# First block of a two-block transformer on one core: the pair stage's jobs, flips and head sums spread over other slots, head factors and key scalings on GpSimd

## The reference

```
h = rms_norm(x) @ w_in       -> h_cq, h_ckv, h_kr, h_dq, h_dk, h_dv, h_gq, h_gk, h_gv
MLA   q_a = rms_norm(h_cq) @ w_uq          6 heads of 64 + 32 (the 32 with rope)
      k_a, v_a = rms_norm(h_ckv) @ w_ukv   keys get the shared rope part h_kr
diff  q_b, k_b, v_b                        4 heads, two 64-wide maps each, values 128 wide
      a = softmax(q0 k0) - lam * softmax(q1 k1);  o_b = rms_norm(a v) * (1 - lambda_init)
GQA   q_c (6 heads), k_c, v_c (2 heads)    axial rope
every q and k of every head: rms_norm(.) * gain, then rope, before the scores
x = x + concat(o_a, o_b, o_c) @ w_o
x = x + (silu(gate) * up) @ w_down,  gate, up = rms_norm(x) @ w_gate_up
```

## Time and profile before

| | us |
|---|---|
| median of three runs | 1777.88 (1773.91 to 1779.11) |
| the profiled execution | 1779.98 |
| its span, first to last instruction | 1778.2 |
| TensorE matmul busy | 1718.4 (97%) |
| VectorE busy | 1198.3 (67%) |
| ScalarE busy | 901.3 (51%) |
| GpSimd busy | 93.9 (5%) |
| mean granted TensorE clock | 0.983 |

### The profile page before, as it was taken

The page is one execution under the profiler, slowest core; times in us unless marked ns, Lnnn a source line. Parts: engine busy times, 40 slices in busy tenths (PEclk is TensorE's granted clock), DMA queues, the critical chain, the costliest instruction groups (busy, mean ns, idle before and its releaser), DMA issues.

```text
span 1778.2 us, 31852 instructions
## 1 busy us (share of the span) xinstructions
PE 1718.4 (97%) x13590; PEld 1655.6 (93%) x13590; DVE 1198.3 (67%) x1752; ACT 901.3 (51%) x1374; POOL 93.9 (5%) x60
## 2 busy tenths in 40 slices
PE   9878999999779999999999999999999999999997
PEld 9867999999769999999999999999999999899997
DVE  5875676647766666367767758984567758769863
ACT  5565544444476444353544765544534545655542
POOL 2000000020000000030000100000200000010000
PEclk9988999999889999999999999999999999999999
DMA  7220565544203654465334434644444345335550
GB/s 279 90 97 13 190 200 186 184 163 151 98 31 129 215 178 166 177 212 176 135 131 166 156 131 157 215 163 160 176 161 163 119 152 191 130 128 193 196 179 35
DMA packets 52830, 274.31 MB, mean 154 GB/s; under 512 B 6096, under 2 KB 6736, under 8 KB 52560
## 3 DMA queue, kind: packets, MB, share of 16 engines
q1 hardware_dynamic: 52544, 271.22, 44.8%
q10 hardware_dynamic: 144, 1.05, 0.2%
HBM read 271.19 MB, written 1.05 MB: 153 GB/s over the span
## 4 chain that ended last, share of the span: by engine, by line
PE 86%; DVE 9%; ACT 2%; issue 2%; ACTq 0%; DVEq 0%
PE bank L774 17%; PE bank L777 17%; PE bank L776 17%; PE scores L774 3%; PE scores L777 3%; PE scores L776 3%; PE bank L783 2%; PE bank L785 2%; PE bank L786 2%; PE heads L774 2%; DVE weights_lo L646 2%; PE heads L776 2%; PE heads L777 2%; PE scores L1094 1%; ACT probs L1167 1%
## 5 line engine op out<-in xcount | busy, mean ns | idle before, releaser
L646 DVE TENSOR_TENSOR weights_lo<-raw,weights_hi 128x1536 fp32r<-128x1536 f32 (+2 forms) x344 | 584.2, 1715 | 257.3 <-ACT weights_hi L635 257.0
L635 ACT ACTIVATE weights_hi<-raw 128x1536 fp32r<-128x1536 f32 (+4 forms) x352 | 499.7, 1438 | 229.0 <-PE bank L777 95.2
L774 PE MATMUL bank<-x_hi,weights_lo 128*128 128x256 f32 (+1 forms) x1600 | 458.9, 287 | 0.4 <-DVE weights_lo L646 0.4
L777 PE MATMUL bank<-x_hi,weights_hi 128*128 128x256 f32 (+1 forms) x1600 | 452.6, 283 | 0.0
L776 PE MATMUL bank<-x_lo,weights_hi 128*128 128x256 f32 (+1 forms) x1600 | 452.5, 283 | 0.0
L774 PEld LDWEIGHTS bank<-x_hi,weights_lo 128*128 128x128 f32 (+1 forms) x1600 | 304.8, 191 | 5.8 <-issue 4.8
L776 PEld LDWEIGHTS bank<-x_lo,weights_hi 128*128 128x128 f32 (+1 forms) x1600 | 304.9, 191 | 2.0 <-issue 2.0
L777 PEld LDWEIGHTS bank<-x_hi,weights_hi 128*128 128x128 f32 (+1 forms) x1600 | 304.9, 191 | 0.0
L776 PE MATMUL bank<-hidden_lo,weights_hi 128*128 128x256 f32 x704 | 198.2, 282 | 0.0
L774 PE MATMUL bank<-hidden_hi,weights_lo 128*128 128x256 f32 x704 | 198.2, 282 | 0.0
L777 PE MATMUL bank<-hidden_hi,weights_hi 128*128 128x256 f32 x704 | 198.2, 282 | 0.0
(11 more groups left out here) (410 smaller groups left out, 3435.3 us busy)
## 6 DMA issues: line engine op xcount, KB each, us to landing
raw<-in_w_b SPq DMA_DIRECT2D x194, 768.0 KB, 4.2
raw<-in_w_a SPq DMA_DIRECT2D x120, 768.0 KB, 4.3
raw<-in_w_a SPq DMA_DIRECT2D x16, 512.0 KB, 3.5
raw<-in_w_b SPq DMA_DIRECT2D x10, 512.0 KB, 4.0
raw<-in_w_b SPq DMA_DIRECT2D x2, 752.0 KB, 4.7
raw<-in_w_a SPq DMA_DIRECT2D x2, 736.0 KB, 8.1
raw<-in_w_b SPq DMA_DIRECT2D x2, 720.0 KB, 4.8
raw<-in_w_a SPq DMA_DIRECT2D x2, 672.0 KB, 7.0
```

Of the source, the lines that this page charges most:

```text
L635: nc.scalar.activation(whi[c % SPLIT][:, 0:n], raw[c % RAW][:, 0:n], ACT.Copy).then_inc(*s.mark("weights_hi", c))
L646: nc.vector.tensor_tensor(wlo[c % SPLIT][:, 0:n], raw[c % RAW][:, 0:n], whi[c % SPLIT][:, 0:n].bitcast(F32), ALU.subtract).then_inc(*s.mar ...
L774: ins = nc.tensor.matmul(dst, wl, xh, start=start, stop=False, skip_group_check=skip)
L777: ins = nc.tensor.matmul(dst, wh, xh, start=False, stop=stop, skip_group_check=skip)
```

## The change

The order of the pair stage is written anew. dv0's values and the splits that belong to its job come before slot 0's pair_in, dv1's values move inside slot 1, the flip of dk1 moves to after slot 1, uk and uq jobs and their ropes move up to one slot ahead, the flips of uk0 to uk2 and uq0 move to after slots 4 and 5, the head sums and the flips of uq1 and uq2 to after slot 6. The uq jobs no longer split chunks ahead; an entry ("chunks", 19) after slot 6 splits chunk 19, so chunk 20 is split with part0's job.

The roots "mla" become two groups, "uk" and "uq". For both, and for the head sums' factor, ScalarE's square root and VectorE's reciprocal go; GpSimd raises the means to the power -0.5 instead, with one `tensor_tensor` against a tile of -0.5. The mean of the head sums is now written by VectorE from PSUM. The three multiplications of MLA keys by their factors go from VectorE to GpSimd. "ready" of an MLA pair is the flip of its queries, which is now the later one. GpSimd waits at the start for VectorE's memsets.

```diff
@@ -470,6 +470,7 @@
         QUIET = place("quiet", 8)
+        HALF = place("minus_half", 16)
         _, na = gain_places(0)
@@ -957,7 +958,7 @@
         QK_NAMES = [q[0] for q in qk_jobs]
-        ROOTS = {"early": (0, 4), "late": (4, 6), "mla": (6, 12)}
+        ROOTS = {"early": (0, 4), "late": (4, 6), "uk": (6, 9), "uq": (9, 12)}
         ROOTS_OF = {name: g for g, (a, b) in ROOTS.items() for name in QK_NAMES[a:b]}
@@ -968,13 +969,13 @@
                     ("job", "dk1"), ("flip", "dk0"), ("scale", "gk"), ("rope", "dq1"), ("flip", "g1"), ("rope", "dk1"), ("job", "dv0"), ("flip", "dq1"),
-                    ("flip", "gk"), ("pair_in", 0), ("roots", "late"), ("scale", "dk1"), ("lambda", 0), ("split", "dv0")]
-        inside = {2: [("rope", "uk0")], 3: [("rope", "uk2")], 4: [("rope", "uq0")], 5: [("rope", "uq2")],
-                  6: [("dif_sum", 0), ("flip", "uq1"), ("flip", "uq2"), ("roots", "mla")] + [("scale", f"uk{i}") for i in range(3)], 7: [("flip", "uk2"), ("dif_spread", 0)],
+                    ("flip", "gk"), ("values", "dv0"), ("pair_in", 0), ("roots", "late"), ("scale", "dk1"), ("lambda", 0)]
+        inside = {1: [("values", "dv1")], 2: [("rope", "uk0"), ("rope", "uk1")], 3: [("rope", "uk2"), ("roots", "uk")] + [("scale", f"uk{i}") for i in range(3)],
+                  4: [("rope", "uq0"), ("rope", "uq1")], 5: [("rope", "uq2")], 6: [("roots", "uq")], 7: [("dif_spread", 0)],
                   12: [("root_table", "o"), ("job", "o3")]}
-        after = {0: [("values", "dv0"), ("flip", "dk1"), ("job", "dv1")], 1: [("values", "dv1"), ("job", "uk0"), ("job", "uk1")], 2: [("rope", "uk1"), ("job", "uk2")],
-                 3: [("job", "uq0"), ("job", "uq1")], 4: [("rope", "uq1"), ("job", "uq2"), ("flip", "uq0")],
-                 6: [("flip", "uk0"), ("flip", "uk1")], 7: [("dif_out", 0)],
+        after = {0: [("job", "dv1")], 1: [("flip", "dk1"), ("job", "uk0"), ("job", "uk1")], 2: [("job", "uk2"), ("job", "uq0")], 3: [("job", "uq1")],
+                 4: [("job", "uq2"), ("flip", "uk0")], 5: [("flip", "uk1"), ("flip", "uk2"), ("flip", "uq0")],
+                 6: [("dif_sum", 0), ("flip", "uq1"), ("flip", "uq2"), ("chunks", 19)], 7: [("dif_out", 0)],
                  8: [("angles", 0), ("job", "part0")], 9: [("job", "part1")], 10: [("job", "part2")]}
@@ -1061,7 +1062,7 @@
                     "v": [(slice(c * 64, c * 64 + 64), lambda kt, h=2 * j + c: MV[:, kt, h * MLA_V:(h + 1) * MLA_V]) for c in range(2)],
-                    "ready": ("qk_flip", f"uk{j}"), "values": ("values", f"uk{j}")}
+                    "ready": ("qk_flip", f"uq{j}"), "values": ("values", f"uk{j}")}
 
@@ -1125,6 +1126,8 @@
                     dve.wait_ge(*s.at(l, "map_exp", 2 * i - 1))
+                if i == DIF_H + GQA_H // 2:
+                    dve.wait_ge(*s.at(l, "by_pool", "uq"))
                 for c in range(2):
@@ -1188,6 +1191,7 @@
         SUMS_BY_ACT = ("dq0", "dk0", "g0")
+        NO_SPLITS = ("uq0", "uq1", "uq2")
 
@@ -1209,7 +1213,9 @@
             ps = start_use(pl, pe, l, f"flip_{name}")
-            if name[1] == "k":
+            if name[:2] == "uk":
+                pe.wait_ge(*s.at(l, "by_pool", name))
+            elif name[1] == "k":
                 pe.wait_ge(*s.at(l, "qk_rope", name))
@@ -1376,12 +1382,7 @@
             st = stage(at)
-            if name[0] == "u":
-                dve.wait_ge(*s.at(l, "qk_raw", name))
-                k = heads_of(st[:, 0:4 * MLA_QK], MLA_QK)
-                f = HFACT[:, i, 0:4].rearrange("p (h x) -> p h x", x=1).to_broadcast([P, 4, MLA_QK])
-                ins = nc.vector.tensor_tensor(k, k, f, ALU.mult)
-            elif name == "gk":
+            if name == "gk":
                 dve.wait_ge(*s.at(l, "qk_sum", job))
@@ -1394,6 +1395,33 @@
             ins.then_inc(*s.mark("qk_rope", name))
+
+        def pool_power(dst, src, half):
+
+            return nc.gpsimd.tensor_tensor(dst, src, half, ALU.pow)
+
+        def pool_factor(pl, pool, l, name):
+
+            s = A
+            a, b = ROOTS[name]
+            pool.wait_ge(*s.at(l, "qk_mean", QK_NAMES[b - 1]))
+            pool_power(HFACT[:, a:b, 0:4], HROOT[:, a:b, 0:4], HALF[:, 0:12].rearrange("p (a n) -> p a n", n=4)).then_inc(*s.mark("by_pool", name))
+
+        def pool_scale(pl, pool, l, name):
+
+            s = A
+            i, at, _ = qk_place(name)
+            pool.wait_ge(*s.at(l, "by_pool", "uk"))
+            pool.wait_ge(*s.at(l, "qk_raw", name))
+            k = heads_of(stage(at)[:, 0:4 * MLA_QK], MLA_QK)
+            f = HFACT[:, i, 0:4].rearrange("p (h x) -> p h x", x=1).to_broadcast([P, 4, MLA_QK])
+            nc.gpsimd.tensor_tensor(k, k, f, ALU.mult).then_inc(*s.mark("by_pool", name))
+
+        def pool_dif_factor(pl, pool, l):
+
+            s = A
+            pool.wait_ge(*s.at(l, "dif_root"))
+            pool_power(OFACT[:, :], OROOT[:, :], HALF[:, :]).then_inc(*s.mark("by_pool", "dif"))
 
@@ -1446,7 +1474,7 @@
                 elif kind == "dif_spread":
-                    pe.wait_ge(*s.at(l, "dif_factor"))
+                    pe.wait_ge(*s.at(l, "by_pool", "dif"))
                     for j in range(2):
@@ -1533,10 +1561,10 @@
                     load_root_table(name)
-                if kind == "split":
-                    split_hi(pl, act, l, pl.last_chunk(name) + 2)
+                if kind == "chunks":
+                    split_hi(pl, act, l, name)
                 if kind == "job":
-                    if name != "dv0":
+                    if name not in NO_SPLITS:
                         split_hi(pl, act, l, pl.last_chunk(name) + 2)
@@ -1565,17 +1593,12 @@
                     nc.scalar.activation(NROOT[:, :], NROOT[:, :], ACT.Sqrt).then_inc(*s.mark("norm_root", "latent"))
-                elif kind == "roots":
+                elif kind == "roots" and name in ("early", "late"):
                     a, b = ROOTS[name]
                     act.wait_ge(*s.at(l, "qk_mean", QK_NAMES[b - 1]))
-                    n = 4 if name == "mla" else 8
-                    nc.scalar.activation(HROOT[:, a:b, 0:n], HROOT[:, a:b, 0:n], ACT.Sqrt).then_inc(*s.mark("qk_root", name))
+                    nc.scalar.activation(HROOT[:, a:b, :], HROOT[:, a:b, :], ACT.Sqrt).then_inc(*s.mark("qk_root", name))
                 elif kind == "pair_out":
                     scalar_pair_out(act, l, name)
-                elif kind == "dif_sum":
-                    act.wait_ge(*s.at(l, "filled", "dif_sum"))
-                    nc.scalar.activation(OROOT[:, :], pl.bank("dif_sum")[:, 0:16], ACT.Sqrt, scale=1.0 / DIF_V, bias=eps_col)\
-                      .then_inc(*s.mark("dif_root"))
                 elif kind == "dif_out":
@@ -1636,10 +1659,10 @@
                           .then_inc(*s.mark("latent_lo", k))
-                elif kind == "split":
-                    split_lo(pl, dve, l, pl.last_chunk(name) + 2)
+                elif kind == "chunks":
+                    split_lo(pl, dve, l, name)
                 elif kind == "job":
-                    if name != "dv0":
+                    if name not in NO_SPLITS:
                         split_lo(pl, dve, l, pl.last_chunk(name) + 2)
@@ -1669,20 +1692,19 @@
                     vector_rope(pl, dve, l, name)
-                elif kind == "roots":
+                elif kind == "roots" and name in ("early", "late"):
                     a, b = ROOTS[name]
                     dve.wait_ge(*s.at(l, "qk_root", name))
-                    n = 4 if name == "mla" else 8
-                    nc.vector.reciprocal(HFACT[:, a:b, 0:n], HROOT[:, a:b, 0:n]).then_inc(*s.mark("qk_factor", name))
-                elif kind == "scale":
+                    nc.vector.reciprocal(HFACT[:, a:b, :], HROOT[:, a:b, :]).then_inc(*s.mark("qk_factor", name))
+                elif kind == "scale" and name[0] != "u":
                     vector_scale(pl, dve, l, name)
...
                 elif kind == "dif_sum":
-                    dve.wait_ge(*s.at(l, "dif_root"))
-                    nc.vector.reciprocal(OFACT[:, :], OROOT[:, :]).then_inc(*s.mark("dif_factor"))
+                    dve.wait_ge(*s.at(l, "filled", "dif_sum"))
+                    nc.vector.tensor_scalar(OROOT[:, :], pl.bank("dif_sum")[:, 0:16], 1.0 / DIF_V, EPS, ALU.mult, ALU.add).then_inc(*s.mark("dif_root"))
                 elif kind == "dif_spread":
@@ -2579,6 +2601,12 @@
                     pool_norm(pl, pool, l, name)
+                elif kind == "roots" and name in ("uk", "uq"):
+                    pool_factor(pl, pool, l, name)
+                elif kind == "scale" and name[0] == "u":
+                    pool_scale(pl, pool, l, name)
+                elif kind == "dif_sum":
+                    pool_dif_factor(pl, pool, l)
                 elif kind == "job":
@@ -2586,6 +2614,7 @@
         def _(pool):
+            pool.wait_ge(*O.at(0, "eps"))
             for l in range(DEPTH):
@@ -2594,6 +2623,7 @@
             nc.vector.memset(QUIET[:, :], 0.0)
```

(1 more changed line is left out.)

## The result

The changed kernel takes **1727.72 us** (1727.05 to 1727.81, 4 runs), the kernel before 1777.3 beside it: a ratio of 0.972, with a 95% interval of 0.971 to 0.974. The gain is 49.6 us, where 40 were forecast, and the time lies under the low end of the range, 1731. The sign and the size of the stage's gain were right; some 10 us came from a place that the prediction had not looked at.

A forecast was written before the change was run, and what follows sets the result against it. TensorE, busy 97% of the span, bounds the kernel; only its waits and slow running can be won. Layer 0's 22 us, less 1 in slots 8 and 9, and layer 1's 19 sum to 40: 1739 us, range 1731 to 1758.

The forecast's parts named there:

- the table of slots: First block's pair stage, layer 0, reworked slot by slot: first scores at 82.0 us, first projection part at 133.65.
- The new wait for chunk 19's split: Slot 7: VectorE waits for ScalarE's put-off split until 125.1 us, splits until 126.8; exponentials and slot 8's scores lose 2 us.
- the schedule without deductions: Layer 0's pair stage by the slot table, before anything comes off: projection starts at 133.65 instead of 159.07, 25.4 us won.
- the 3.5 set aside for handovers and GpSimd: Deductions in the pair stage: 1.5 us for handovers over eight slots, 2 us for VectorE delayed beside GpSimd.
- the upper bound: Cost of one GpSimd power, which had no row: at most 3.1 us, the longest single addition; 0.7 was taken.
- the first sign in my list of what would be wrong: Pair stage: TensorE waiting for GpSimd before the flip of uk0 or the spread of the head factors; no size given.
- The memset, and GpSimd's wait for it, lie under the first loads and cost nothing: Kernel start: setting the tile of exponents, and GpSimd's wait for that, are hidden under the first loads; cost nothing.
- no delay on DVE: Best case of the range, pair stage: GpSimd delays VectorE by nothing and handovers are short; gain 47 us, 1731 us.
- GpSimd as delay on DVE: Rival, pair stage: GpSimd's work blocks VectorE, 6 to 12 us per layer lost; gain 18 to 33 us; chance 0.24.
- The far dearer power: Rival, slots 4 and 7: a GpSimd power costs so much that the kernel gets slower, 1796 us at 14; chance 0.07.
- 3p − 13.7: Loss per layer in us from p = 7.4 on, p being a power's time; eats 20 us at p = 11.
- The chain that closes again: Rival, slots 1 to 5: slot 0's 11.2 us return as waits, leaving 11 per layer from slots 6 and 7, 1758; chance 0.05.

The follow-up runs named there:

- pad_only: The kernel before with one unused 64-byte tile where the change puts its tile of exponents, no instruction added or moved; 1766.36 us, ratio 0.994.
- realign: The changed kernel with a second unused 64-byte tile behind the new one, so tiles behind it start 128 bytes later than before the change; 1741.12 us, ratio 0.980.
- slot0_only: The kernel before with only the first two slots' part of the change (value copies, chunk split, flip of dk1); 1760.02 us, ratio 0.990.

## Why the prediction was wrong in size and right in kind

*The stage.* Against the table of slots, the lengths are: slot 0 7.0 us (6.95 forecast), slots 1 to 5 29.8 (27.9), slot 6 5.8 (5.9), slot 7 7.7 (7.1), slot 8 3.8 (3.8). Layer 0 gained 22.9 where 22 stood in the sum, layer 1 19.6 where 19 stood. The new wait for chunk 19's split came as named: VectorE stood 2.02 us for it, up to 127.56. TensorE's waits of 1.47 and 1.32 us in slots 1 to 5 were forecast as 1.6 and 1.2. In all, layer 0's stage took 54.2 us where the schedule without deductions had 51.7 (133.65 less 82.0): 2.5 us, of the 3.5 set aside for handovers and GpSimd. From the stage's end to GpSimd's first addition of squares it is 40.9 us in layer 0 instead of 39.1, 1.7 us lost where 1 was forecast, and 36.5 in layer 1 instead of 37.1.

*GpSimd.* Two errors nearly cancelled. A power took 2.28 us for 12 columns and 2.90 for 16, near the upper bound and not the 0.7 that I took; I had placed it by its few columns, and four more of them cost 0.62 us. GpSimd was busy for 9.85 us per layer and not 5.1. But slack hid it, up to the 0.96 us at the spread, the first sign in my list of what would be wrong. And GpSimd beside VectorE cost almost nothing. GpSimd's power and scalings, with the one VectorE operation that they stretched, and then the last power with VectorE's split, all in layer 0:
```profile
106.20 2.28 POOL L1401 TENSOR_TENSOR head_factor<-head_root,minus_half 128x12 f32<-128x12 f32 x1 [79.12 <-DVE head_root L1349]
108.56 2.40 POOL L1418 TENSOR_TENSOR qk<-qk,head_factor 128x384 f32<-128x384 f32 x3
108.75 0.66 DVE L1136 TENSOR_TENSOR row<-row,head_factor 128x2 f32<-128x2 f32 x1
...
125.62 2.90 POOL L1401 TENSOR_TENSOR dif_factor<-dif_root,minus_half 128x16 f32<-128x16 f32 x1 [5.29 <-DVE dif_root L1707]
127.56 1.76 DVE L647 TENSOR_TENSOR weights_lo<-raw,weights_hi 128x1536 fp32r<-128x1536 f32 x1 [2.02 <-ACT weights_hi L636]
```
The row-by-factor product beside the scalings took 0.66 us instead of 0.16 (0.65 in layer 1). That is 0.5 us, where I took 2 and the nearest rows gave up to 5.1. Those rows pair large additions with VectorE operations that read two SBUF inputs; here the operations beside GpSimd are mostly maxima, sums and products out of PSUM. The lock of the Trainium skill, "SBUF — State Buffer", section "Who interferes with whom", had made the sum 6 us smaller when taken over all of GpSimd's time. The trace shows 0.5, and most of VectorE's work here is not of the kind that the section names. The stretched product is, with two inputs from SBUF, and ended at 109.41, as the first scaling did (0.80 us from 108.56). But the split, with two as well, took 1.76 us beside the power and 1.75 in the kernel before with GpSimd idle: a power that had begun did not hold it up.

*The step that failed* is "The memset, and GpSimd's wait for it, lie under the first loads and cost nothing". It priced the instructions of the new tile and not its place. Nothing was nearly right for the instructions: layer 0's first scores start at 82.19 us instead of 81.99. But the same 64 bytes without any instruction gave 9.8 us (pad_only), and with the hidden vectors back on a multiple of 128 bytes the kernel took 1741.12 us, 2 above the forecast (realign). What the sum put at nothing was worth a gain of 10. Why the tiles' distance sets a matmul's pace stays open. No rival held this, and the range ended at "no delay on DVE", 47 us, because all its cases lay in the stage.

*The rivals.* GpSimd as delay on DVE: 0.5 us per layer, where this rival needed 6. The far dearer power: 2.28 us lay within the slack worked out for the keys (4 us), and 2.90 lay 0.7 over the slack behind the head sums (2.2 us), where TensorE did wait 0.96. The rival's formula let losses begin at 4 us for a power and left out this nearer slack, which the prediction itself had named. How it comes to 3p − 13.7 from 7.4 us on can't be followed from its text, and no run had so dear a power. The chain that closes again: refuted by slot0_only, which keeps 8 to 11 us per layer.

## What to carry to other kernels

A change that adds or moves a tile is two changes: compare the matmuls of untouched code by group, and run the old kernel with the empty tile alone before the gain is put down to the schedule. A root on ScalarE can cost more than its two table loads when it waits between them (some 15 us here), since all behind it in the list stands still; a slow operation on an idle engine is cheap for as long as its consumer has slack. Where layout matters, the moving tile's distance from the weights is worth a sweep over a few multiples of 64 bytes, with several executions of each: one trace can have caught either of two paces.

## What was not expected of the hardware

The pace of 128 x 256 float32r matmuls depends on the distance of the two SBUF tiles that are read: 390 in 46 us at 384 bytes modulo 512, 408 at 448. At 448 and at 192 bytes a stretch went at one of two paces (179 or 172 matmuls in 20 us at 448), and executions of one such kernel spread over 16 to 20 us. GpSimd's power of a 128 x 16 tile takes 2.90 us, of a 128 x 12 tile 2.28, and a 128 x 384 multiplication by a broadcast factor 0.80.
